# Reordering the front of a fused transformer step on Trainium2: x and modulation loads interleaved, five subtractions moved to GpSimd, zero products ahead of the constants

## The chip, the cores and the metric

The kernel runs on one core of one Trainium2 chip. Its time is the device time of one execution in microseconds (us), and the number to predict is the median over several executions. The engines are called by the profile's short names: PE is TensorE (PEld its weight loads), DVE is VectorE, ACT is ScalarE, POOL is GpSimd, SP is the engine that issues most DMAs. A name with q (ACTq, SPq) is an engine's instruction queue, as it issues a DMA.

## The reference, cut to what matters

One layer of a hybrid network over 640 tokens (128 context and 512 latent tokens) of width 1024, all in float32. The stages that the change touches are these:

```
m = silu(cond) @ w_mod + b_mod              # 2 conditionings, 1024 x 6144: shift, scale, gate (twice)
u = layer_norm(x) * (1 + scale) + shift     # 640 x 1024
z = u @ w_in                                # 1024 x 2816: q, k, v, recurrence, gate, Hyena
h = sin(freq0 * (feats @ w1 + b1))          # Hyena's filters: feats 640 x 33, w1 33 x 64
h = sin(freq1 * (h @ w2 + b2))              # w2 64 x 64
filters = (h @ w3) * exp(-t * |decay|)      # w3 64 x 1024; forward and backward half
spectrum = real Fourier transform of the circular filters
```

Behind them come the convolutions in the frequency domain, a recurrence, attention, the output projection and a mixture of 16 experts. They fill the time from about 65 us to the end and are the same in both kernels.

## The kernel before, in words

The core's engines run one hand-ordered program each; semaphores tie them together. Everything lives in one SBUF array called `arena`, so most names in the profile are `arena`; PSUM banks are called `bank`.

The front, up to about 65 us, does four things at once.

- **The filters.** PE makes layer 0 (`filter_layer(0)`, L1426, 33 rows by 64 columns), DVE folds its argument to the sine's range (`filter_fold`, L2052 to L2058), ACT takes the sine (L976), PE makes layer 1 (L1422), then fold and sine again. PE then makes five tiles of filter rows (`filter_rows`, L1456) into ten places in PSUM banks, some of them used twice. For each tile DVE runs `filter_parts(a)` (L2087 to L2100): the near half times a window into `EV`, the far half times a window into `OD`, after which `eo_win` counts one up, then EV = near + far and OD = near - far. Tiles 1 and 0 of the token order also get one more addition on a single partition (`skip`, L2100). The order of tiles is `FILTER_ORDER = (1, 2, 3, 4, 0)`.
- **The spectra.** `spectrum(g, odd)` (L1477) is two products of 128x128 by 128x512; DVE combines the halves in `spectrum_far` and `spectrum_near` (L2110, L2115).
- **The modulation.** SP loads eight blocks of `w_mod` (1024 KB each) through three buffers, and PE multiplies each block in `mod1(k)` (L1410). After the last one ACT and DVE copy the four result rows out of PSUM (L1013, L2142; semaphore `m1_ev`), and PE transposes them (L1525).
- **The normalisation.** `x_moments(i)` (L2077 to L2079) makes the mean and variance of token tile i on DVE, as soon as its rows have landed. ACT takes roots and scales x. PE transposes x (`ut`, L1438 and L1444), ACT applies scale and shift (L1021) and rounds to a high half (L1026), and DVE makes the low half (`u_low`, L2157).

PE's engine would be idle between these products, so `front_dense(n)` (L1491) inserts n products of the identity with constants; their results are never read. The first product of the input projection (`m = 0`, L1574 and L1575) waits per k for `u_low(k)`. GpSimd makes the low half of each weight piece (`low_half`, L772) from about 47 us on and has nothing to do between 3 and 47 us.

DVE waits in its own order: `filter_fold(0)`, `x_moments(0)`, `x_moments(1)`, `filter_fold(1)`, `x_moments(2..4)`, `filter_parts(0)`, `filter_parts(1)`, two tiny operations on the moments, `filter_parts(2..4)`. PE's `filter_rows([(3, 1)])` waits for `eo_win` 2, since the banks that it writes are read by `filter_parts` 0 and 1.

On the queues: SP issues `consts`, the five tiles of x, then the blocks of `w_mod`; ACT issues `filt` (features, w1 and w2 in one table of 128 partitions), `decay`, twice `hy_w3` and `skip`, later the transform's table `dft_taps`.

Of the kernel before, what the change touches and what calls it, by code (L numbers as in the profile page):

```python
# [9 lines left out]
P = 128  # L10
# [57 lines left out]
def build(nc, t):  # L68
# [8 lines left out]
    with ctx:  # L77
# [160 lines left out]
        filt = fl.take(NTOK + HIDDEN + P)  # L238
        feats, w1, w2 = filt[:, 0:NTOK], filt[:, NTOK:NTOK + HIDDEN], filt[:, NTOK + HIDDEN:NTOK + HIDDEN + P]
# [123 lines left out]
        mod_in = [sem(f"mod_in{i}") for i in range(3)]  # L363
        mod1_mm = sem("mod1_mm")
# [114 lines left out]
        modc_in = sem("modc_in")  # L479
# [21 lines left out]
        mod1_buf = [arena[:, MTAT:MTAT + 2048], arena[:, MTAT + 2048:MTAT + 4096], flat[1]]  # L501
        mod2_buf = [flat[1], flat[2], flat[0]]

        def wait_w_in(eng, p):

            eng.wait_ge(win_in[p % 2], 16 * (p // 2 + 1))
# [31 lines left out]
        def _(eng):  # L538
# [6 lines left out]
            for i in range(TT):  # L545
                eng.dma_start(X[:, i, :], t["x"][i * P:(i + 1) * P, :]).then_inc(ld_x[i], 16)
# [9 lines left out]
            def mod1_block(k):  # L556
                if k >= 3:
                    eng.wait_ge(mod1_mm, k - 2)
                eng.dma_start(mod1_buf[k % 3], t["w_mod"][k * P:(k + 1) * P, 0:2048]).then_inc(mod_in[k % 3], 16)
# [16 lines left out]
            for k in range(KT):  # L576
                mod1_block(k)
# [167 lines left out]
        def _(eng):  # L745
# [20 lines left out]

            def low_half(m):
# [175 lines left out]
        def _(eng):  # L943
# [11 lines left out]
            eng.dma_start(filt, t["filt"]).then_inc(ld_filt, 16)  # L955
# [55 lines left out]
            eng.wait_ge(eo_rdy, TT)  # L1011
            for g in range(2):
                S.activation(mrow1[g], mod_rows(B[4], g), ACT.Copy).then_inc(m1_ev, 1)  # L1013
# [390 lines left out]
        def _(eng):  # L1404
# [8 lines left out]
            def mod1(k):  # L1413

                eng.wait_ge(mod_in[k % 3], 16 * (k // 3 + 1))
                mod_block(B[4], k, mod1_buf[k % 3]).then_inc(mod1_mm, 1)

            def filter_layer(layer):
# [4 lines left out]
                else:  # L1423
                    eng.wait_ge(ld_filt, 16)
# [22 lines left out]
            eng.wait_ge(ld_const, 16)  # L1447
# [13 lines left out]
            def spectrum(g, odd):  # L1461
# [11 lines left out]
                else:  # L1473
                    eng.wait_ge(eo_win, (3, 3, 4)[g - 1])
                src, bank = (OD if q else EV), (odd_bank if odd else even_bank)[g]
# [5 lines left out]
            def ctx_spectrum():  # L1481

                eng.wait_ge(eo_rdy, TT)
                eng.wait_ge(half_ev, 4)
# [3 lines left out]
            def front_dense(n):  # L1488

                for b in range(n):  # L1490
                    mm(B[5][:, :], ident, consts[:, 2 * KT:2 * KT + 512], start=True, stop=True)  # L1491
# [25 lines left out]
            mod1(6)  # L1517
            mod1(7)
            spectrum(1, 1)
# [73 lines left out]
            def mod2(b):  # L1593

                eng.wait_ge(mod_in[b % 3], 16 * ((3, 3, 2)[b % 3] + b // 3 + 1))
# [431 lines left out]
        def _(eng):  # L2027
# [15 lines left out]
            ts_(cond, sig, 0.5, None, ALU.mult).then_inc(modc_in, 1)  # L2043
            after(modc_in)
# [36 lines left out]
            def filter_parts(a):  # L2081
# [5 lines left out]
                tt_(EV[:, i, :], b0[:, :], WN[:, i, 0:512], ALU.mult)  # L2087
                if i < 2:

                    stt(OD[:, i, :], b1[:, :], col("not0"), WN[:, i, 512:1024], ALU.mult, ALU.mult).then_inc(eo_win, 1)  # L2090
# [874 lines left out]
```

## Time and profile before

| | us |
|---|---|
| median of 3 runs | 634.93 (634.59 to 637.37) |
| the profiled execution, its own time | 633.17 |
| its span, first to last instruction | 631.3 |
| PE busy in the span | 600.8 |
| DVE, ACT, POOL busy | 440.5, 305.6, 188.4 |

The span begins with the first instruction of any engine. The profiled execution took 1.87 us more than its span. Times below are from the span's start.

### The profile page before, as it was taken

What the parts mean: (1) busy time and instruction counts of PE and PEld (TensorE: products, weight loads), DVE (VectorE), ACT (ScalarE), POOL (GpSimd) and SP (SyncE); (2) the same over time, 40 slices, a digit from 0 to 9 for tenths busy, and PEclk for the clock granted to TensorE, in tenths of its full rate; (3) what the DMA queues carried; (4) which work ended last, traced back from release to release, by engine and by line L of the source; (5) the groups of instructions that cost most, each with busy time, mean ns of one, the idle gap of its engine ahead of it and who ended that gap; (6) DMA issues with size and microseconds to landing.
All of it is one profiled execution on the core that took longest, in us unless ns stands there. A gap on an engine that the chain in (4) does not pass through costs nothing.

```text
span 631.3 us, 9327 instructions
## 1 busy us (share of the span) xinstructions
PE 600.8 (95%) x3353; PEld 455.3 (72%) x3353; DVE 440.5 (70%) x757; ACT 305.6 (48%) x506; POOL 188.4 (30%) x152
## 2 busy tenths in 40 slices
PE   6899999999999988998999999989999999999994
PEld 2237999999999965557888888747767677676352
DVE  4967766834994654467553499988998877983187
ACT  2748122335344543005795342846565655752354
POOL 1002333345551307041496070421212221321121
PEclk9999999999999999999999999999999999999998
DMA  9985852222221269764980706769999999999788
GB/s 305 387 305 222 305 186 97 101 101 100 101 68 66 92 238 325 303 264 99 290 271 36 294 8 234 280 168 370 393 376 403 390 388 406 374 364 372 291 299 144
DMA packets 40040, 154.89 MB, mean 245 GB/s; under 512 B 7049, under 2 KB 17033, under 8 KB 27451
## 3 DMA queue, kind: packets, MB, share of 16 engines
q1 hardware_dynamic: 27912, 115.41, 50.6%
q10 hardware_dynamic: 5522, 23.48, 9.4%
q0 software_dynamic: 6560, 15.42, 8.3%
q8 instruction: 27, 0.44, 0.3%
q14 instruction: 19, 0.15, 0.1%
HBM read 141.59 MB, written 23.63 MB: 262 GB/s over the span
## 4 chain that ended last, share of the span: by engine, by line
PE 82%; DVE 7%; DMA 5%; ACT 4%; issue 2%; POOL 0%; DVEq 0%; ACTq 0%; POOLq 0%
PE bank L1898 13%; PE bank L1574 12%; PE bank L1575 12%; PE bank L1770 9%; PE bank L1952 8%; PE bank L1410 3%; PE bank L1747 2%; PE bank L1674 2%; PE bank L1880 2%; DMA arena<-in_w_mod 2%; PE bank L1477 2%; PE bank L1625 2%; PE bank L2011 2%; PE bank L1730 2%; DMA u_scr<-arena 1%
## 5 line engine op out<-in xcount | busy, mean ns | idle before, releaser
L772 POOL TENSOR_TENSOR w_low<-arena,w_high 128x1024 fp32r<-128x1024 f32 x22 | 53.6, 2437 | 145.9 <-ACT w_high L971 145.9
L2544 DVE TENSOR_TENSOR gate_up_low<-arena,gate_up_high 128x1024 fp32r<-128x1024 f32 x64 | 75.3, 1221 | 12.3 <-ACT gate_up_high L1256 10.2
L1256 ACT ACTIVATE gate_up_high<-arena 128x1024 fp32r<-128x1024 f32 x64 | 63.9, 1054 | 15.5 <-DMA arena<-in_moe_w_gu 15.5
L971 ACT ACTIVATE w_high<-arena 128x1024 fp32r<-128x1024 f32 x22 | 23.2, 1058 | 87.8 <-PE bank L1575 87.0
L1574 PE MATMUL bank<-u_high,w_high 128*128 128x320 f32 x176 | 56.3, 320 | 1.7 <-DVE u_low L2157 1.7
L1952 PE MATMUL bank<-arena 128*128 128x512 f32 x128 | 57.7, 593 | 0.0
L1575 PE MATMUL bank<-u_high,w_low 128*128 128x320 f32 x176 | 54.4, 309 | 0.0
L1574 PE MATMUL bank<-u_high,w_low 128*128 128x320 f32 x176 | 54.4, 309 | 0.0
L1574 PE MATMUL bank<-u_low,w_high 128*128 128x320 f32 x176 | 54.4, 309 | 0.0
L1575 PE MATMUL bank<-u_low,w_high 128*128 128x320 f32 x176 | 54.4, 309 | 0.0
L1575 PE MATMUL bank<-u_high,w_high 128*128 128x320 f32 x176 | 54.4, 309 | 0.0
L1898 PE MATMUL bank<-gate_up_high,xt_high 128*128 128x512 f32 x128 | 51.4, 402 | 0.5 <-DVE xt_low L2696 0.5
L1898 PE MATMUL bank<-gate_up_low,xt_high 128*128 128x512 f32 x128 | 50.0, 391 | 0.0
L1898 PE MATMUL bank<-gate_up_high,xt_low 128*128 128x512 f32 x128 | 50.0, 390 | 0.0
L902 POOL DMA_INDIRECT y_scr<-arena,store_rows x16 | 17.7, 1108 | 84.2 <-DVE arena L2710 79.7
L1952 PEld LDWEIGHTS bank<-arena 128*128 128x128 f32 x128 | 23.2, 190 | 23.1 <-issue 23.0
L895 POOL DMA_INDIRECT arena<-u_scr,tokens x18 | 19.6, 1087 | 59.1 <-PE bank L1880 49.6
L1574 PEld LDWEIGHTS bank<-u_high,w_high 128*128 128x128 f32 x176 | 33.1, 188 | 2.9 <-DVE u_low L2157 2.6
L1575 PEld LDWEIGHTS bank<-u_high,w_high 128*128 128x128 f32 x176 | 33.1, 188 | 0.2 <-issue 0.2
L1574 PEld LDWEIGHTS bank<-u_low,w_high 128*128 128x128 f32 x176 | 33.0, 188 | 0.0
L1574 PEld LDWEIGHTS bank<-u_high,w_low 128*128 128x128 f32 x176 | 33.0, 188 | 0.0
L1575 PEld LDWEIGHTS bank<-u_low,w_high 128*128 128x128 f32 x176 | 33.0, 188 | 0.0
(442 smaller groups left out, 1396.4 us busy)
## 6 DMA issues: line engine op xcount, KB each, us to landing
arena<-in_moe_w_gu SPq DMA_DIRECT2D x38, 1024.0 KB, 10.1
arena<-in_w_mod SPq DMA_DIRECT2D x24, 1024.0 KB, 6.6
arena<-in_moe_w_down ACTq DMA_DIRECT2D x13, 1024.0 KB
arena<-in_w_in SPq DMA_DIRECT2D x11, 1024.0 KB, 4.8
arena<-in_moe_w_down SPq DMA_DIRECT2D x6, 1024.0 KB
y_scr<-arena SPq DMA_DIRECT2D x11, 512.0 KB, 9.1
arena<-in_x SPq DMA_DIRECT2D x10, 512.0 KB, 9.6
arena<-y_scr SPq DMA_DIRECT2D x10, 512.0 KB, 6.0
```

Of the source, the lines that this page charges most:

```text
L772: G.tensor_tensor(WL[s_][:, :, w], ring[s_][:, :, w], WH[m % 2].bitcast(F), ALU.subtract).then_inc(wl_rdy, 1)
L895: eng.indirect_dma_start(xg[j], None, u_scr, bass.IndirectOffsetOnAxis(ap=which, axis=0), bounds_check=NTOK - 1, oob_is_err=False).then_in ...
L902: eng.indirect_dma_start(y_scr, bass.IndirectOffsetOnAxis(ap=stores[:, n:n + 1], axis=0), yy[n % 2], None, bounds_check=2 * NTOK, oob_is_e ...
L971: S.activation(WH[m % 2], ring[(m // 2) % 2][:, :, (m % 2) * P:(m % 2 + 1) * P], ACT.Copy).then_inc(wh_rdy, 1)
L1256: S.activation(WGH[j][c], raw_gu[s][:, c, :, :], ACT.Copy).then_inc(wgh_rdy, 1)
L1410: last = mm(bank[32 * g:32 * g + 32, :], cond32[k], w[:, 512 * g:512 * (g + 1)], start=(k == 0), stop=(k == KT - 1))
L1574: mm(B[1 + m % 2][:, 0:HALF], w, u[k][:, HALF:NTOK], start=first, stop=end)
L1575: last = mm(B[3 + m % 2][:, 0:HALF], w, u[k][:, 0:HALF], start=first, stop=end)
L1770: last = mm(B[2 * (i % 2) + b][:, :], x[j][:, k, :], w[p][c][:, k % 2, :], start=(k == 0 and q == 0), stop=(k == KT - 1 and q == 2))
L1898: last = mm(B[j][:, :], x[j][:, k, :], w[k // 2][:, k % 2, :], start=(k == 0 and q == 0), stop=(k == KT - 1 and q == 2))
L1952: last = mm(B[4 + b][:, :], hT[j][:, k, :], raw_dn[s][:, k, b * 512:(b + 1) * 512], start=(k == 0), stop=(k == 1))
L2544: tt_(WGL[s][c], raw_gu[s][:, c, :, :], WGH[j][c].bitcast(F), ALU.subtract).then_inc(wgl_rdy, 1)
```

## The change

- SP's order: x tile 0, `w_mod` block 0, x tiles 1 and 2, block 1, x tiles 3 and 4, blocks 2 to 7. Five buffers instead of three (`mod1_buf`). The first two pieces of `w_in` wait for five and eight products of `mod1` (before: none and six).
- `filt` becomes 33 partitions by 704 columns, and w2 a transfer of its own (`hy_w2`, 128x128).
- `filter_parts` works in place in the window array `WN`, DVE keeps the sum, and the difference goes to GpSimd, with a new semaphore `od_rdy`.
- `x_moments(1)` comes after `filter_fold(1)`.
- PE begins with `front_zero(4)`: four products of the array ZERO with itself, 256 columns each, after the first `pads`; the wait for the constants stands behind them. Each f32 product is two records in the trace. `front_dense` is 3, 2 and (into bank 0, after `eo_win` 1) 1 instead of 1, 4 and 4. Each `mod1(0..2)` moves one place earlier; `mod1(7)` comes after `spectrum(1, 1)` instead of before it.
- At the end of `m = 0`, `u_low(6)` no longer stands behind `spectrum_far(3)`, nor `u_low(7)` behind `spectrum_near(3)`.

```diff
-        mod1_buf = [arena[:, MTAT:MTAT + 2048], arena[:, MTAT + 2048:MTAT + 4096], flat[1]]
+        mod1_buf = [arena[:, MTAT:MTAT + 2048], arena[:, MTAT + 2048:MTAT + 4096], flat[1], flat[2], flat[0]]
...
             eng.dma_start(consts, t["consts"]).then_inc(ld_const, 16)
-            for i in range(TT):
-                eng.dma_start(X[:, i, :], t["x"][i * P:(i + 1) * P, :]).then_inc(ld_x[i], 16)
...
             def mod1_block(k):
-                if k >= 3:
-                    eng.wait_ge(mod1_mm, k - 2)
+                if k >= 5:
+                    eng.wait_ge(mod1_mm, k - 4)
...
             def w_in_piece(p):
-                if p == 1:
-                    eng.wait_ge(mod1_mm, 6)
+                if p < 2:
+                    eng.wait_ge(mod1_mm, 8 if p else 5)
...
-            for k in range(KT):
+            for i in range(TT):
+                x_rows(i)
+                if i in (0, 2):
+                    mod1_block(i // 2)
+            for k in range(2, KT):
                 mod1_block(k)
...
+            for a in range(TT):
+                i = FILTER_ORDER[a]
+                eng.wait_ge(eo_win, a + 1)
+                G.tensor_tensor(OD[:, i, :], WN[:, i, 0:512], WN[:, i, 512:1024], ALU.subtract).then_inc(od_rdy, 1)
...
-            eng.dma_start(filt, t["filt"]).then_inc(ld_filt, 16)
+            eng.dma_start(filt[0:FEATS, :], t["filt"]).then_inc(ld_filt, 16)
+            eng.dma_start(w2, t["hy_w2"]).then_inc(ld_filt, 16)
...
-            front_dense(1)
+            front_zero(4)
+            eng.wait_ge(ld_const, 16)
             filter_layer(0)
-            front_dense(4)
+            front_dense(3)
             filter_layer(1)
-            eng.wait_ge(modc_in, 1)
-            front_dense(4)
+            eng.wait_ge(cond_rdy, 2)
+            mod1(0)
+            front_dense(2)
             eng.wait_ge(filt_sin, 2)
             eng.wait_ge(ld_tables, 64)
             filter_rows([(0, 0), (1, 1)])
-            mod1(0)
+            mod1(1)
             eng.wait_ge(filt_read, 2)
             filter_rows([(2, 1), (4, 0)])
-            mod1(1)
+            mod1(2)
+            eng.wait_ge(eo_win, 1)
+            front_dense(1, 0)
             eng.wait_ge(eo_win, 2)
             filter_rows([(3, 1)], 2)
-            mod1(2)
             spectrum(0, 0)
...
             spectrum(0, 1)
             mod1(6)
+            spectrum(1, 1)
             mod1(7)
-            spectrum(1, 1)
...
-                tt_(EV[:, i, :], b0[:, :], WN[:, i, 0:512], ALU.mult)
+                near, far = WN[:, i, 0:512], WN[:, i, 512:1024]
+                tt_(near, b0[:, :], near, ALU.mult)
...
-                    tt_(OD[:, i, :], b1[:, :], WN[:, i, 512:1024], ALU.mult).then_inc(eo_win, 1)
+                    tt_(far, b1[:, :], far, ALU.mult).then_inc(eo_win, 1)
                 after(eo_win)
-                step(tt_(EV[:, i, :], EV[:, i, :], OD[:, i, :], ALU.add))
-                if i < 2:
-                    eng.wait_ge(ld_tables, 64)
-                last = stt(OD[:, i, :], OD[:, i, :], -2.0, EV[:, i, :], ALU.mult, ALU.add)
+                last = tt_(EV[:, i, :], near, far, ALU.add)
                 if i < 2:
                     step(last)
+                    eng.wait_ge(ld_tables, 64)
                     last = tt_(EV[0:1, i, :], EV[0:1, i, :], skip[0:1, :], ALU.add)
...
-            x_moments(1)
             filter_fold(1)
-            for i in range(2, TT):
+            for i in range(1, TT):
                 last = x_moments(i)
...
-                if k == 7:
-                    spectrum_far(3)
             u_low(KT - 2)
+            spectrum_far(3)
+            u_low(KT - 1)
             spectrum_near(3)
-            u_low(KT - 1)
```

## Rows read from the trace of the kernel before

**Rows 1.** The page: busy time, share of the span, and instructions of PE, PEld, DVE.
```profile
PE 600.8 (95%) x3353; PEld 455.3 (72%) x3353; DVE 440.5 (70%) x757; ACT 305.6 (48%) x506; POOL 188.4 (30%) x152
```

**Rows 2.** The chain that ended last, 0 to 80 us: start, length, what.
```profile
0.72 3.98 DMA arena<-in_consts
...
8.29 5.74 PE bank L1491 x8
...
22.15 0.69 DVE arena L2087
...
27.04 1.98 PE bank L1456 x4
...
30.02 1.91 PE bank L1477 x4
...
42.38 1.85 PE bank L1410 x16
...
46.14 0.35 PE bank L1525 x16
```

**Rows 3.** DMA issues between 3.8 and 4.5 us: count, size, median time to landing.
```profile
arena<-in_w_mod SPq DMA_DIRECT2D x1, 1024.0 KB, 16.6
...
arena<-in_w_mod SPq DMA_DIRECT2D x2, 1024.0 KB, 17.8
```

**Rows 4.** Stretches: engines' busy time, clock, DMA share, last column GB/s.
```profile
0.00:21.20 21.20, 15.98 (x40) 5.76 (x40) 12.62 (x30) 7.88 (x10) 1.70 (x17) 1.00 0.93 336
...
15.60:25.50 9.90, 9.42 (x38) 2.73 (x36) 9.49 (x19) 7.59 (x9) 0.00 (x0) 1.00 1.00 425
```

**Rows 5.** Timelines of SP's queue and of DVE up to 26 us: start, length.
```profile
3.89 34.05 SPq L559 DMA_DIRECT2D arena<-in_w_mod  x8
...
8.41 0.68 DVE L2052 TENSOR_SCALAR arena<-bank,arena 128x384 f32<-128x384 f32 x1 [2.28 <-PE bank L1426]
...
17.80 0.69 DVE L2077 BATCH_NORM_STATS2 arena<-arena 128x6 f32<-128x512 f32 x1
...
23.53 0.69 DVE L2094 TENSOR_TENSOR arena<-arena 128x512 f32<-128x512 f32 x1
...
24.98 0.68 DVE L2100 TENSOR_TENSOR arena<-arena 1x512 f32<-1x512 f32 x1
```

**Rows 6.** Timeline, stretches in which POOL and DVE both work.
```profile
47.37 4.68 POOL L772 TENSOR_TENSOR w_low<-arena,w_high 128x1024 fp32r<-128x1024 f32 x2 [44.36 <-ACT w_high L971]
...
47.69 0.69 DVE L2115 TENSOR_TENSOR arena<-arena,bank 128x512 f32<-128x512 f32 x1
...
111.66 2.42 POOL L772 TENSOR_TENSOR w_low<-arena,w_high 128x1024 fp32r<-128x1024 f32 x1 [5.17 <-ACT w_high L971]
...
111.78 2.31 DVE L2296 TENSOR_TENSOR arena<-arena 128x4 f32<-128x4 f32 x1
```

**Rows 7.** Groups of POOL instructions by line and shape: busy us, mean ns.
```profile
L803 POOL TENSOR_TENSOR arena<-arena 128x1024 f32<-128x1024 f32 x8 | 18.8, 2355 | 21.6 <-DMA arena<-in_rpb 21.5
...
L815 POOL TENSOR_TENSOR arena<-arena 128x256 f32<-128x256 f32 x10 | 7.3, 728 | 0.8
```

**Rows 8.** Timeline of PEld, front_dense(4): start, length.
```profile
11.79 0.34 PEld L1491 LDWEIGHTS bank<-arena 128*128 128x128 f32 x1 [0.52 <-issue]
12.58 0.19 PEld L1491 LDWEIGHTS bank<-arena 128*128 128x128 f32 x1 [0.45 <-issue]
```

**Rows 9.** Timeline, around the last mod1 block and the spectrum's halves.
```profile
42.51 0.69 DVE L2110 TENSOR_TENSOR arena<-arena,bank 128x512 f32<-128x512 f32 x1 [4.55 <-PE bank L1477]
...
44.37 1.42 DVE L2142 COPY arena<-bank 2x512 f32<-2x512 f32 x2 [0.45 <-PE bank L1410]
```

**Rows 10.** Timeline at the end of m = 0.
```profile
61.44 0.74 ACT L1026 ACTIVATE u_high<-arena 128x640 fp32r<-128x640 f32 x1
...
62.45 0.82 DVE L2157 TENSOR_TENSOR u_low<-arena,u_high 128x640 fp32r<-128x640 f32 x1
...
64.79 0.19 PEld L1574 LDWEIGHTS bank<-u_high,w_high 128*128 128x128 f32 x1 [0.58 <-DVE u_low L2157]
```

More of the change, by code:

```diff
@@ L237, in build @@
         HF, FA, FB = (fl.take(SPAN) for _ in range(3))
-        filt = fl.take(NTOK + HIDDEN + P)
-        feats, w1, w2 = filt[:, 0:NTOK], filt[:, NTOK:NTOK + HIDDEN], filt[:, NTOK + HIDDEN:NTOK + HIDDEN + P]
+        filt = fl.take(NTOK + HIDDEN)
+        feats, w1 = filt[:, 0:NTOK], filt[:, NTOK:NTOK + HIDDEN]
+        w2 = fl.take(P)
         decay = fl.take(D)
@@ L363, in build @@
         mod_in = [sem(f"mod_in{i}") for i in range(3)]
+        mod1_in = mod_in + win_in
         mod1_mm = sem("mod1_mm")
@@ L478, in build @@
         scalar_st = sem("scalar_st")
-        modc_in = sem("modc_in")
+        od_rdy = sem("od_rdy")
         eo_win = sem("eo_win")
@@ L556, in mod1_block @@
             def mod1_block(k):
-                if k >= 3:
-                    eng.wait_ge(mod1_mm, k - 2)
-                eng.dma_start(mod1_buf[k % 3], t["w_mod"][k * P:(k + 1) * P, 0:2048]).then_inc(mod_in[k % 3], 16)
+                if k >= 5:
+                    eng.wait_ge(mod1_mm, k - 4)
+                eng.dma_start(mod1_buf[k % 5], t["w_mod"][k * P:(k + 1) * P, 0:2048]).then_inc(mod1_in[k % 5], 16)
             def w_in_piece(p):
-                if p == 1:
-                    eng.wait_ge(mod1_mm, 6)
+                if p < 2:
+                    eng.wait_ge(mod1_mm, 8 if p else 5)
                 elif p >= 2:
@@ L1011, in _ @@
             eng.wait_ge(eo_rdy, TT)
+            eng.wait_ge(od_rdy, TT)
             for g in range(2):
@@ L1474, in spectrum @@
                     eng.wait_ge(eo_win, (3, 3, 4)[g - 1])
+                if q:
+                    eng.wait_ge(od_rdy, 4 if odd else 2)
                 src, bank = (OD if q else EV), (odd_bank if odd else even_bank)[g]
@@ L1483, in ctx_spectrum @@
                 eng.wait_ge(eo_rdy, TT)
+                eng.wait_ge(od_rdy, TT)
                 eng.wait_ge(half_ev, 4)
@@ L1486, in ctx_spectrum, with front_dense, front_zero @@
                 mm(B[3][:, :], TAPSc[1], OD[:, 0, :], start=True, stop=True).then_inc(spec_mm, 1)
-            def front_dense(n):
+            def front_dense(n, bank=5):
                 for b in range(n):
-                    mm(B[5][:, :], ident, consts[:, 2 * KT:2 * KT + 512], start=True, stop=True)
-            front_dense(1)
+                    mm(B[bank][:, :], ident, consts[:, 2 * KT:2 * KT + 512], start=True, stop=True)
+            def front_zero(n):
+                eng.wait_ge(pads, 1)
+                for b in range(n):
+                    mm(B[5][:, 0:256], ZERO[:, 0:P], ZERO[:, 0:256], start=True, stop=True)
+            front_zero(4)
+            eng.wait_ge(ld_const, 16)
             filter_layer(0)
-            front_dense(4)
+            front_dense(3)
             filter_layer(1)
-            eng.wait_ge(modc_in, 1)
-            front_dense(4)
+            eng.wait_ge(cond_rdy, 2)
+            mod1(0)
+            front_dense(2)
             eng.wait_ge(filt_sin, 2)
@@ L2042, in _ @@
             step(stt(sig, sig, 1.0, cond, ALU.add, ALU.mult))
-            ts_(cond, sig, 0.5, None, ALU.mult).then_inc(modc_in, 1)
-            after(modc_in)
+            ts_(cond, sig, 0.5, None, ALU.mult).then_inc(cond_rdy, 1)
+            eng.wait_ge(cond_rdy, 2)
             magic = 1.5 * 2.0 ** 23
@@ L2140, in _ @@
             eng.wait_ge(mod1_mm, KT)
+            eng.wait_ge(od_rdy, TT)
             for g in range(2, 4):
@@ L2909 @@
     pair2[0:HIDDEN, 0:HIDDEN] = pair2[HIDDEN:P, HIDDEN:P] = a["hy_w2"][0]
-    filt = np.zeros((P, NTOK + HIDDEN + P), f32)
-    filt[0:FEATS, 0:NTOK] = features()
-    filt[0:FEATS, NTOK:NTOK + HIDDEN] = a["hy_w1"][0]
-    filt[:, NTOK + HIDDEN:] = pair2
+    filt = np.concatenate([features(), a["hy_w1"][0]], 1).astype(f32)
     rgw = np.zeros((P, 8, P), f32)
```

17 lines of the change are left out of this document (9 added, 8 removed).

## The prediction

> **What bounds the kernel now.** I read the page first, then the chain that ended last for the first 80 us, then the timelines of the engines in that stretch, then the DMA issues. PE is busy for 95% of the span [rows 1], and nothing behind 65 us is edited, so only what the front does to the start of the projections counts. The reader should see three stretches in the chain [rows 2]: until 14 us PE (the constants at 4.70, then among others eight filler records that end at 14.03 and hold up layer 1); until 27.04 DVE, which has no gap; and from 27.04 to 46.14 PE again, 19.10 us without a gap. Behind it, ACT's chain over eight values of k and DVE's low halves set the end of m = 0 [rows 10]. I sum the change as a shift of each of these marks.
>
> **Where DVE starts its filter parts (T0, before 22.15) [rows 2].** In the new order DVE does four tiles of moments after the second fold, and the last needs x tile 4. Three tiles took 17.80 to 22.15 without a gap [rows 2, 5], so one takes 1.45, and nothing waited for x.
>
> - By engines alone: POOL's first memsets end about 2 us into the span. Four zero products are eight records of 256 columns. The eight filler records of 512 columns took 5.74 [rows 2]: about five at 0.86 and three at 0.43, since PE's records became twice as fast between the loads at 11.79 and 12.58 [rows 8], near 12.4. So 256 slow columns are 0.43, the zeros 3.4 us, to 5.5. Layer 0 takes 1.5 more (constants plus filler to the next filler, 4.70 to 8.29, less 2.07), a fold and sine 3.7 (the fold began at 8.41 [rows 5]; the sine was done near 12.0), so layer 1 could run at 10.7 and end at 11.5 if PE is fast by then. A fold of 3.1 and four tiles of 5.8 give T0 = 20.4. If PE stays slow until 12.4 as before, three fillers (5.2 us) end at 12.3, layer 1 at 13.1, and T0 = 22.0.
> - By the queue: x tile 4 now stands behind two blocks of w_mod. Exactly the same bytes of SP's queue (constants, five tiles, two blocks) were through when the second block landed before. The first block was issued at 3.89 [rows 5] and took 16.6, the median of the first two is 17.8 [rows 3], so the second, issued some 0.35 later, took 19.0 and landed at about 23.2. The filter's table shrinks from 416 KB to 91, plus 64 for w2: 261 KB less, 0.6 us at 425 GB/s [rows 4]. Late bound: 22.6. The early bound counts bytes only: SP's 5.0 MB and ACT's 2.1 MB make 7.1 MB, which the DMA engines had moved by 21.2 [rows 4]. I take the middle, 21.9; with 1.45 for its moments T0 = 23.35.
>
> The later of the two decides: T0 moves by +1.2. The earlier filter layers, the zero products among them, are then hidden behind the wait for x tile 4; if x came in time they would be worth the 1.6 between 22.0 and 20.4.
>
> **DVE and POOL (eo_win 2, before 27.04).** Before, near, far, sum, difference, skip row, near, far took 4.87 from T0. Sum and difference together took 1.45 from 23.53 to 24.98 [rows 5]; without the difference it is 4.87 - 0.72 = 4.15. But POOL's subtraction runs at the same time. Its duration is not in the trace; between 728 ns for 256 columns and 2355 for 1024 [rows 7] 512 columns are 1.27. And DVE stands still meanwhile: while POOL worked from 111.66 to 114.08, a DVE addition of four columns took 2.31 and ended at 114.09; one that reads PSUM took its usual 0.69 at 47.69, within a POOL operation from 47.37 on [rows 6]. So products with a bank are free, the sum and the skip row are not. After far, DVE's own next instruction starts within some 0.04 (0.69 of a step of 0.72 is work), while POOL must be woken by another engine's semaphore. So I let DVE have the sum first, POOL follows, and the skip row waits for its end: about 1.2 us more, once before eo_win 2. If POOL went first, the cost is the same once, and 0.6 to 1.3 for each later tile, where PE is the bound and hides it. The bounds are 0 and 1.3; I take 1.15, since the nearest rows are unambiguous. From T0 to eo_win 2: 5.3 instead of 4.87, +0.4. So eo_win 2 comes at 28.65, +1.6.
>
> The Trainium skill speaks against this part too: its page GPSIMD Engine Reference, section Specifications, says that GpSimd shares its SBUF interfaces with VectorE, with contention for DVE instructions that have two SBUF inputs or run in a two-port mode. It gives no price. The four-column addition of 2.31 us [rows 6] agrees; with the rule but a price of nothing the sum would come out 1.15 lower, with the rows it is as above.
>
> **PE from eo_win 2 to the transposes (before 19.10) [rows 2].** mod1(2) now stands ahead of the wait: its block is behind x tile 4 in the queue, about 24.5 to 25, and the filler of 0.86 follows it, so both end before 28.65: -1.0. spectrum(1, 1) comes after one block of mod1 instead of two, and needs DVE's two halves of spectrum 0, the first of which began at 42.51 and took 0.69, after a product that ended at 42.38 [rows 2, 9]: 1.6 from that end, against 0.93 of mod1(6): +0.65, and the 0.93 of mod1(7) goes behind it. There the rows' copies follow: from mod1(7)'s end at 44.23 DVE copied until 45.79 [rows 2, 9], hidden by 1.91 of spectrum(1, 1); now nothing is left to hide them, and PE waits about 1.7. In all: rows 1.98, spectra and blocks to the end of spectrum(0, 1) 12.4 (30.02 to 42.38 [rows 2]), then 1.6, 1.9, 0.9, 1.7 = 20.45, +1.35. The marks behind shift by 1.6 + 1.35 = +2.95. The waits for od_rdy cost nothing: POOL's second difference is done about 3 us after eo_win 2, and the first odd product comes 5 us after it.
>
> **The end of m = 0.** Before, u_low(6) stood behind spectrum_far(3), and u_low(7) behind both halves, so k = 7 began on PE at 64.79 [rows 10]. ACT had its last high half at 62.18 (61.44 + 0.74), and with 0.82 for u_low(7) [rows 10] and 0.06 for the wake-up PE could begin at 63.06: -1.73. PE's own products reach this point at about 63.2, and start a little earlier relative to ACT than before, since u_low(0) no longer runs beside POOL's second low half. So I count the whole -1.73; if PE is the later one it is -1.6.
>
> **Edits at nothing.** The semaphore under mod1(0) is another name for the same event. SP's five buffers, the waits of w_in (piece 0 is issued after five blocks, as late as before, and wanted 3 us later; piece 1 some 5 us later than before, but not wanted until m = 0 has ended near 66 [rows 10]) and the move of filter fillers are hidden; if a w_in piece were late, ACT's high half would wait for it.
>
> **Sum.** +2.95 - 1.73 = +1.2. The profiled execution's own time is 633.17, of which 631.3 is span; the change would make it 634.4. The median shown is 1.76 above it, and on that scale the forecast is 634.93 + 1.2 = 636.1. Its own bounds: x tile 4 between 21.2 and 22.6 is -0.7 and +0.7, POOL's price -1.15 and +0.15, the copies +-0.3: 634.0 to 637.5.
>
> **Rivals.** (a) *The x tiles come in time*, because the small ACT transfers are shorter and share less. T0 = 20.4, eo_win 2 at 25.7, shift -1.35 + 1.35 = 0, and the sum is -1.7: 633.2, or 632.1 if POOL's price falls away too. For it: DVE and PE stand ready. Against it: the position in the queue. (b) *POOL costs nothing* with x late: +0.05, 635.0. Against it speak the rows cited. (c) *PE falls back to the slow level*, the rival on the slower side. The granted clock reads 1.00 throughout [rows 4], yet the filler's records took 0.86 until about 12.4 and 0.43 after it, which is the step from 1.2 to 2.4 GHz [rows 2, 8]; PE had been busy from 4.7 until it rose. Before, PE was busy for 9.42 of the 9.90 us from 15.60 on [rows 4]. Now I expect two gaps of about 2.5 us, from 17.4 to the landing of block 1 near 19.9 and from 22.3 to eo_win 1 near 24.7. If the clock falls there and needs as long as at the start, 7.7 us at half speed cost 3.85 behind eo_win 2: +5.1, 640.0. It decides when the level is still low at eo_win 2; a fall that is over by then costs nothing. For it: the gaps; against it: block 1 and the filler after eo_win 1 lie between. (d) *The zero products don't raise the clock.* T0 is then 22.0 by engines, still before 23.35: the same 636.1, and in case (a) 634.8.
>
> **Chances.** Forecast, with (d) in it, 0.48; (a) 0.24; (b) 0.12; (c) 0.11; 0.05 for others of either sign. About 0.5%, 3.2 us, is what a measurement of this kernel tells from no change. Of (a) and the rest 0.07 go below -3.2 us; of (c), the forecast's tail and the rest 0.13 go above +3.2. So 0.80 for no difference. The range from 632.3 to 638.6 leaves out about 0.08 below and 0.12 above.
>
> **What would show it.** Right: x tile 4 lands between 21 and 23, DVE has a gap before its last moments, and filter_parts(0) starts near 23; the two skip rows on DVE take 1.8 us instead of 0.68; PE waits 1.5 or more before L1525; u_low(6) and u_low(7) precede the halves of spectrum 3, with no wait of PE over 0.3 near the end of m = 0. Wrong: no wait for x, sums on DVE unchanged beside POOL, or records of 0.86 after 20 us.

## The result, and the profile after

| | before | after |
|---|---|---|
| median, 10 runs each on the same chip | 635.19 (633.47 to 637.37) | 639.33 (637.28 to 644.42) |
| ratio after/before, 95% interval | | 1.0069 (1.005 to 1.0087) |
| the profiled execution, its own time | 633.17 | 639.24 |
| its span | 631.3 | 637.2 |
| mean granted clock of the profiled execution | 0.997 | 0.99 |
| mean granted clock over all its executions (before: the 85 of the experiments) | 0.993 | 0.989 |

The change makes the kernel 4.1 us slower. The forecast was +1.2, and its range ended at 638.6. The engines' busy time on the page hardly differs from [rows 1]; only POOL has 10 us more:

```profile
PE 602.2 (95%) x3355; PEld 456.4 (72%) x3355; DVE 438.5 (69%) x752; ACT 305.5 (48%) x506; POOL 199.0 (31%) x157
```

The loss is mostly in waiting, and the same marks as before show where (us from the start of the span; k = 7 is the last product pair of m = 0):

| mark | before | forecast | after |
|---|---|---|---|
| T0, first `filter_parts` | 22.15 | 23.35 | 24.66 |
| eo_win 2 | 27.0 | 28.65 | 29.7 |
| third tile of filter rows | 27.04 | 28.65 | 30.8 |
| transposes of the modulation rows | 46.1 | 49.0 | 51.4 |
| k = 7 of m = 0 | 64.79 | 66.0 | 68.61 |

At k = 7 the kernel is 3.8 us behind, nearly all of the median's 4.1. The two profiled spans differ by 5.9; but the execution of before that was profiled lies 2.0 under its own median and that of after only 0.1. The other 2 us come behind m = 0, where the programs are the same: from k = 7 to PE's last product it takes 557.1 us before and 559.0 after, at a clock of 1.00 in both. In the profiles of the experiments this stretch takes between 556.2 and 559.8, so 2 us is within what single executions scatter.

The chain of work that ended last, from the first DMA issue to k = 7 (start, length, what), is to be held against [rows 2]:

```profile
3.72 17.96 DMA arena<-in_x
21.70 0.69 DVE arena L2102
...
24.66 0.69 DVE arena L2113
...
26.07 1.42 PE bank L1469 x2
...
30.84 1.91 PE bank L1469 x4
...
48.71 1.04 PE bank L1424 x8
49.83 0.69 DVE arena L2166
50.55 0.71 DVE arena L2166
51.39 0.41 PE bank L1550 x16
...
68.65 0.37 PE bank L1599
```

Before, the constants and PE's fillers led this chain. Now a transfer of x does, issued at 3.72 and landed at 21.70. It is x tile **3**; tile 4, issued at 4.3, follows 18.6 us later, near 22.9. Two tiles of moments (2.9 us) then stand between the landing and T0. The timeline of DVE shows the wait, the moments, and what became of sum and skip row:

```profile
21.70 0.69 DVE L2102 BATCH_NORM_STATS2 arena<-arena 128x6 f32<-128x512 f32 x1 [1.79 <-DMA arena<-in_x]
...
24.66 0.69 DVE L2113 TENSOR_TENSOR arena<-bank,arena 128x512 f32<-128x512 f32 x1
...
26.05 0.69 DVE L2120 TENSOR_TENSOR arena<-arena 128x512 f32<-128x512 f32 x1
26.77 1.63 DVE L2124 TENSOR_TENSOR arena<-arena 1x512 f32<-1x512 f32 x1
...
49.83 1.42 DVE L2166 COPY arena<-bank 2x512 f32<-2x512 f32 x2 [3.18 <-PE bank L1424]
```

The skip row takes 1.63 us instead of 0.68 [rows 5], beside POOL's difference:

```profile
26.10 1.76 POOL L777 TENSOR_TENSOR arena<-arena 128x512 f32<-128x512 f32 x1 [23.09 <-DVE arena L2116]
```

POOL's record ends at 27.86, DVE's at 28.40, 0.54 behind it: the row began at 26.77, and the records look as if it did its work once POOL was done. This is the lock that the prediction described.

PE's granted clock in stretches of 5 us (after the stretch and its length: busy time of PE, PEld, DVE, ACT, POOL, then the clock, the DMA share and GB/s):

```profile
10.00:15.00 5.00, 5.00 (x15) 1.56 (x14) 4.35 (x9) 0.52 (x1) 0.00 (x0) 0.69 1.04 315
20.00:25.00 5.00, 2.53 (x14) 0.68 (x6) 3.19 (x7) 4.98 (x7) 0.00 (x0) 1.00 1.03 428
25.00:30.00 5.00, 3.93 (x11) 1.00 (x12) 4.86 (x7) 0.89 (x2) 1.96 (x2) 0.68 1.01 428
30.00:35.00 5.00, 5.00 (x14) 1.51 (x16) 4.79 (x9) 3.31 (x3) 3.36 (x2) 0.98 1.01 426
```

Before, the clock read 1.00 throughout [rows 4], and on to PE's last product. (It reads 1.00 in the slow start of either program too; there the length of the records tells.) Now PE falls to the low level twice, and each fall has an idle stretch ahead of it. The timeline of PE has both:

```profile
2.07 3.78 PE L1513 MATMUL bank<-arena 128*128 128x256 f32 x8 [2.07 <-POOLq L768]
7.90 0.86 PE L1440 MATMUL bank<-arena 33*64 33x384 f32 x4 [2.05 <-DMA arena<-in_hy_w]
...
26.07 1.42 PE L1469 MATMUL bank<-arena 64*128 64x512 f32 x2 [3.54 <-DVE arena L2116]
27.41 1.94 PE L1424 MATMUL bank<-arena 128*32 128x512 f32 x8
29.28 1.55 PE L1507 MATMUL bank<-arena 128*128 128x512 f32 x2
30.77 0.69 PE L1469 MATMUL bank<-arena 64*128 64x512 f32 x1
```

The first idle stretch is new: the zero products end at 5.85, and layer 0 then waits 2.05 us for w2, which is now a transfer of its own in the same semaphore. In the seven other kernels with this table, profiled once each, layer 0 began between 5.75 and 6.25, so this stretch belongs to this one execution. The second lasts 3.54 us, while DVE waits for x. Behind it mod1(2) takes 1.94 and the filler 1.55, where 1.0 and 1.1 are usual, so the third tile of filter rows starts 1.05 us after the bank that it wants is free.

### The profile page after: what moved, and what is told of

Read it like the earlier page. It is cut to its first block, busy times and chain, and to the rows that moved or that the text cites. A ratio compares the mean times of both kernels' runs of the same rounds, so it can differ in the third digit from the quotient of the medians.

```text
span 637.2 us, 9336 instructions
## 1 busy us (share of the span) xinstructions
PE 602.2 (95%) x3355; PEld 456.4 (72%) x3355; DVE 438.5 (69%) x752; ACT 305.5 (48%) x506; POOL 199.0 (31%) x157
## 4 chain that ended last, share of the span: by engine, by line
PE 73%; DMA 13%; DVE 7%; ACT 4%; issue 3%; SPq 0%; DVEq 0%; POOL 0%; POOLq 0%; ACTq 0%
PE bank L1599 12%; PE bank L1600 12%; PE bank L1923 11%; PE bank L1795 9%; PE bank L1977 6%; DMA arena<-in_w_mod 3%; PE bank L1424 3%; DMA arena<-in_x 3%; DMA arena<-in_moe_w_gu 2%; PE bank L1772 2%; PE bank L1699 2%; PE bank L1492 2%; PE bank L1905 2%; PE bank L2036 2%; DVE gate_up_low L2567 1%
## 5 line engine op out<-in xcount | busy, mean ns | idle before, releaser
L914 POOL DMA_INDIRECT y_scr<-arena,store_rows x16 | 18.6, 1160 | 89.0 <-DVE arena L2733 82.7
## 6 DMA issues: line engine op xcount, KB each, us to landing
arena<-in_moe_w_gu SPq DMA_DIRECT2D x38, 1024.0 KB, 13.5
arena<-in_moe_w_down SPq DMA_DIRECT2D x6, 1024.0 KB, 10.9
```

The lines of the kernel that those rows point to most:

```text
L914: eng.indirect_dma_start(y_scr, bass.IndirectOffsetOnAxis(ap=stores[:, n:n + 1], axis=0), yy[n % 2], None, bounds_check=2 * NTOK, oob_is_e ...
```

## The experiments

x_first, warm, mod7_ahead and no_zeros ran on one chip together; tail_only, zeros_tail, mixed and no_pool on a second; warm_mod7, zeros_only and ones_lead on a third. The medians of the kernel before on the three were 635.11, 635.18 and 635.28 (27 to 29 runs each). Ratios are to it; marks are from one profiled execution of each kernel. An interval of a ratio is 1.1 to 1.7 us wide to either side, so of two kernels of the table a difference under about 2 us isn't established by the medians alone.

| kernel | median | ratio (95%) | mean clock | T0 | transposes | k = 7 |
|---|---|---|---|---|---|---|
| x_first | 636.41 | 1.0011 (0.9988 to 1.0035) | 0.9887 | 21.33 | 48.95 | 66.17 |
| warm | 638.51 | 1.0062 (1.0041 to 1.0083) | 0.9918 | 24.48 | 50.23 | 68.27 |
| mod7_ahead | 637.17 | 1.0043 (1.0017 to 1.0069) | 0.9877 | 24.49 | 49.97 | 67.2 |
| warm_mod7 | 634.16 | 0.9983 (0.996 to 1.0006) | 0.9935 | 24.53 | 47.69 | 64.93 |
| mixed | 632.41 | 0.9961 (0.9942 to 0.998) | 0.9937 | 20.75 | 44.91 | 62.13 |
| no_zeros | 638.65 | 1.0068 (1.0041 to 1.0095) | 0.9891 | 24.47 | 51.19 | 68.41 |
| no_pool | 638.92 | 1.0064 (1.0042 to 1.0085) | 0.9893 | 24.42 | – | – |
| tail_only | 633.69 | 0.9983 (0.9959 to 1.0008) | 0.9928 | 22.10 | 47.62 | 65.30 |
| zeros_only | 632.96 | 0.996 (0.9934 to 0.9986) | 0.9936 | 20.89 | 46.47 | 65.22 |
| ones_lead | 633.48 | 0.998 (0.9955 to 1.0005) | 0.9939 | 20.76 | 44.69 | 63.66 |
| zeros_tail | 631.59 | 0.9942 (0.9926 to 0.9959) | 0.9941 | 20.18 | 44.11 | 61.55 |

The mean clock needs care, since it counts stretches in which the level costs nothing. Behind PE's last product the level falls in every profile; the last stretch of before, then of after:

```profile
625.00:631.30 6.30, 0.00 (x0) 0.00 (x0) 2.35 (x4) 1.02 (x3) 0.00 (x0) 0.65 0.76 166
630.00:637.20 7.20, 0.00 (x0) 0.00 (x0) 3.03 (x7) 1.53 (x3) 0.35 (x1) 0.56 0.67 146
```

PE has no product in either. One minus the clock, times the length of the stretch, is the full-speed time that the low level takes: 2.2 us here before and 3.2 after, from 2 to 3.2 in all the kernels. The same sum over the stretches up to 80 us tells of the front: 0 in the profiles of before, zeros_tail, ones_lead, mixed and warm_mod7; 1.7 in tail_only, zeros_only, warm and no_zeros; 3.4 in after, x_first and mod7_ahead; 8.5 in no_pool.

### x_first: is it the place in the queue?

After, with all of x ahead of the blocks, and mod1(0) to mod1(2) at their old places on PE.

```diff
             for i in range(TT):
                 x_rows(i)
-                if i in (0, 2):
-                    mod1_block(i // 2)
-            for k in range(2, KT):
+            for k in range(KT):
                 mod1_block(k)
```

> The changed kernel with the five x tiles ahead of all blocks of w_mod, and with mod1(0), mod1(1), mod1(2) back at their old places, since their blocks land later. Theory 1 (the late x tiles hold DVE): no wait of DVE for x, filter_parts(0) begins near 21 instead of 24.66, the third row tile (L1469 after eo_win 2) near 26.5 instead of 30.77, the transposes near 48 (the third block is back behind the rows, +1.0), and the time is 2.5 to 3.5 us under the changed kernel's, about 1 above that of before. Rival (something else, such as POOL's lock or the clock, makes the front late): filter_parts(0) earlier, but the rows after eo_win 2 not before 29.

The median is 2.9 us under that of after, and k = 7 comes 2.4 us earlier. DVE no longer waits for x, and T0 comes 3.3 us earlier. But now the first block is late. PE's timeline and the stretch around it:

```profile
20.70 1.94 PE L1422 MATMUL bank<-arena 128*32 128x512 f32 x8 [1.79 <-DMA arena<-in_w_mod]
...
20.00:25.00 5.00, 4.30 (x16) 1.24 (x16) 4.86 (x7) 4.47 (x6) 1.76 (x1) 0.58 1.01 426
```

PE stood idle from 14.2 to 16.2 and from 18.9 to 20.7 and fell to the low level near 17.4, between the two, this time ahead of eo_win 2 instead of behind it. The mean clock over the runs, 0.9887, is as low as that of after. So the place of x in the queue, with the places of the three blocks on PE that go with it, is worth about 3 us here, and with x in time the rest of the change is still no gain.

### warm: fill PE's second gap

```diff
             eng.wait_ge(filt_read, 2)
+            front_dense(4, 6)
             filter_rows([(2, 1), (4, 0)])
```

> The changed kernel with four more filler products (into bank 6) ahead of filter_rows 2 and 4, so that PE isn't idle in front of the first eo_win. Theory 2 (PE's low level after idle time costs about 1 us): the granted clock stays at 1.00 from 20 us on, the row tile, block and filler after the first eo_win take about 2.8 us instead of 4.7, the third row tile starts at eo_win 2 (29.8) instead of 30.77, and the time is 1.0 us lower. Rival (the low level costs nothing, since DVE is the later one): clock 1.00, but the third row tile still near 30.8 and the same time.

It gains 0.8 us, within the intervals. The fillers do what they are for: the clock holds at 1.00 from 20 to 50 us, and the third tile of filter rows starts at 29.61, 1.2 earlier. Then the level falls elsewhere. In PE's stretch behind the transposes:

```profile
50.00:55.00 5.00, 4.77 (x30) 3.32 (x31) 2.26 (x8) 3.50 (x5) 4.03 (x2) 0.68 0.89 264
```

PE had waited 1.69 us for the rows' copies, with mod1(7)'s end ahead of it, and the level fell near 51.8, some 1.6 us after PE had started again. x's transposes then ran at half speed:

```profile
50.23 0.42 PE L1551 MATMUL bank<-arena 2*128 2x2 f32 x16 [1.69 <-DVE arena L2167]
...
53.38 1.92 PE L1458 MATMUL bank<-arena 128*128 128x128 f32 x8
```

### mod7_ahead: give the rows' copies their cover back

```diff
+            mod1(7)
             spectrum(1, 1)
-            mod1(7)
```

> The changed kernel with mod1(7) ahead of spectrum(1, 1) again. Theory 3 (the uncovered copies of the modulation rows and the wait for DVE's halves cost 2.3 us): PE has no gap of over 0.3 us between spectrum(0, 1) and the transposes, these start 2.3 to 2.5 us earlier (near 49.0 instead of 51.39), and the time is 2.3 us lower. Rival (the later marks absorb it, as ACT's high halves wait for w_in or for PE anyway): the transposes come earlier, but the first product of m = 0 moves by less than 1.

It gains 2.2 us, and the intervals of the two just overlap. From the third tile of filter rows to the transposes it takes 18.21 us instead of 20.62, since no wait is left there:

```profile
46.20 1.92 PE L1424 MATMUL bank<-arena 128*32 128x512 f32 x16
48.05 1.98 PE L1492 MATMUL bank<-arena 128*128 128x512 f32 x4
49.97 0.41 PE L1550 MATMUL bank<-arena 2*128 2x2 f32 x16
```

mod1(6) and mod1(7) run together, spectrum(1, 1) hides the copies, and the transposes follow without a gap. In its profile the level was low for longer at the same place as in after, 25 to 35 us, which is why the transposes came at 49.97 and not near 49.0:

```profile
25.00:30.00 5.00, 4.11 (x11) 0.94 (x12) 4.86 (x7) 0.00 (x0) 2.13 (x2) 0.53 1.02 429
30.00:35.00 5.00, 5.00 (x9) 1.77 (x10) 4.29 (x8) 3.49 (x4) 3.18 (x2) 0.79 1.02 429
```

### warm_mod7: both repairs of PE, x still late

The two edits above together.

> The changed kernel with both repairs on PE's side, the four fillers ahead of filter_rows 2 and 4 and mod1(7) ahead of spectrum(1, 1); x tiles stay late. If the three causes add up, the third row tile starts near 29.6, the transposes near 47.8, and the time is 3.3 to 3.5 us under that of the changed kernel, near 636.0. What is left between it and the kernel of x tiles first with the same order at the end of the blocks (632.4) is then the late x tiles, 3.5 us. Rival (PE idle behind mod1(7) and the low level are the same loss seen twice): 637 as with mod1(7) alone.

T0 is as late as in after (24.53), and yet the kernel takes 634.16, which is 5.2 us less than after and not to be told from before. The level does not fall; of the stretches from 20 to 55 us the two that fell above now read

```profile
25.00:30.00 5.00, 4.45 (x19) 1.26 (x16) 4.86 (x7) 0.00 (x0) 2.09 (x2) 1.00 1.01 428
...
50.00:55.00 5.00, 5.00 (x34) 3.96 (x33) 2.72 (x5) 4.78 (x7) 2.96 (x2) 1.00 1.04 385
```

This run shows that most of the loss can be had back while x stays late. It doesn't show that late x is free: the kernel keeps the new end of m = 0, which tail_only puts at 1.5, and only with that does it come out level with before. At k = 7 it is 3.7 us ahead of after: 0.1 from T0, 1.0 from there to the third row tile, 2.6 from there to the transposes. The mean clock rises from 0.989 to 0.9935 (0.0045 of 639 is 2.9 us, part of it where it costs nothing), and the way from the third row tile to the transposes shortens from 20.62 to 18.04. The expectation was 636.0, so the gain is larger than forecast. Alone the two repairs gained 0.8 and 2.2; that together they gain 2.2 more than this sum is in line with the traces (with either alone the level still fell in the front), but the four medians have uncertainties of 1.2 to 1.7 each, so the excess itself is not established.

### mixed: x in time as well

x_first and mod7_ahead together, x_moments(1) ahead of `filter_fold(1)` as before, and two more fillers behind layer 1:

```diff
-            front_dense(2)
+            front_dense(4)
...
             x_moments(0)
+            x_moments(1)
             filter_fold(1)
-            for i in range(1, TT):
+            for i in range(2, TT):
```

> The changed kernel without the parts that the runs so far showed to cost: x tiles ahead of the blocks, mod1(0..2) at their old places, mod1(7) ahead of spectrum(1, 1), x_moments(1) between the folds, four fillers behind layer 1. The zeros, five buffers, the small filter table, POOL's differences, the filler after eo_win 1 and the new end of m = 0 stay. If the causes are the late x tiles, the order at the end of the blocks and the low level, filter_parts(0) begins near 20.5, the third row tile near 25.6, the transposes near 44.8, and the time is 2.5 to 3 us under that of before (ratio 0.9955). Rival (a cause not found stays in): not faster than before.

632.41, faster than before. Against warm_mod7, whose clock is the same, this leaves 1.7 us for the late x and the few places on PE and DVE that go with it, where 3.5 were expected. The intervals of the two overlap; the marks put k = 7 at 62.13 against 64.93, 2.8 earlier.

### no_zeros: after without the leading products

```diff
-            front_zero(4)
             eng.wait_ge(ld_const, 16)
```

> The changed kernel without its four zero products: PE begins with layer 0, when the w2 table has landed near 7.9. Theory 4 (the zero products raise PE's level before layer 0, but the gain is hidden behind the x tiles): layer 0 takes 1.5 us instead of 0.86, layer 1 ends some 0.5 to 1 later, DVE still waits for x tile 3 at 21.7, filter_parts(0) begins at 24.7 as before, and the time is that of the changed kernel within 0.5 us. Rival (the zeros do nothing to the level): layer 0 takes 0.86 all the same. Second rival (the early start costs: an early rise lets the level fall again before 13 us): the products at 26 to 31 us run at the high level now, and the time is 1 us lower.

638.65: no difference from after. Layer 0 runs at 5.75 and at half speed, layer 1 ends near 13.5, and still T0 is 24.47, because x tile 3 lands as late:

```profile
5.75 1.54 PE L1440 MATMUL bank<-arena 33*64 33x384 f32 x4 [5.75 <-DMA arena<-in_hy_w]
```

Here layer 0 has to wait for the same transfer, but to 5.75, not 7.90. When w2 lands varies from one execution to another: in mod7_ahead, whose program is that of after up to 40 us, layer 0 began at 5.78 right behind the zeros.

### no_pool: the differences back on DVE

```diff
-            for a in range(TT):
-                i = FILTER_ORDER[a]
-                eng.wait_ge(eo_win, a + 1)
-                G.tensor_tensor(OD[:, i, :], WN[:, i, 0:512], WN[:, i, 512:1024], ALU.subtract).then_inc(od_rdy, 1)
...
-                last = tt_(EV[:, i, :], near, far, ALU.add)
+                step(tt_(EV[:, i, :], near, far, ALU.add))
+                last = stt(OD[:, i, :], far, -2.0, EV[:, i, :], ALU.mult, ALU.add)
...
                 after(eo_rdy)
+                eng.sem_inc(od_rdy, 1)
```

> The changed kernel with the five differences back on DVE, everything else as it is. Theory 5 (POOL's lock gives back what the moved work saves): the skip row takes 0.68 instead of 1.63 and the difference 0.72, so from filter_parts(0) to eo_win 2 it is 4.9 instead of 5.1, DVE ends its last tile some 2 us later than now, which PE does not wait for, and the time is that of the changed kernel within 0.5 us. Rival (the lock is a main part of the loss): the time falls by 1 us or more.

638.92 against 639.33: the same. From T0 to eo_win 2 it is 5.02 us, with POOL it was 5.06. DVE's timeline for the first tile, against that of after above:

```profile
26.53 0.69 DVE L2117 SCALAR_TENSOR_TENSOR arena<-arena 128x512 f32<-128x512 f32 x1
27.26 0.68 DVE L2121 TENSOR_TENSOR arena<-arena 1x512 f32<-1x512 f32 x1
28.15 0.69 DVE L2109 TENSOR_TENSOR arena<-bank,arena 128x512 f32<-128x512 f32 x1 [0.21 <-DVE arena L2121]
```

The difference costs 0.69 on DVE, and the skip row is back at 0.68. From the first near product to that of the next tile it is 3.73 us; with POOL it was 3.78. The lock is real, and in this tile it eats the whole of what the move saved. It doesn't in every tile: where DVE's next work reads a bank, as in after's third tile, the near products of two tiles are 2.05 us apart (31.63 to 33.68) and were 2.78 before. But there PE is the later one. (The profiled execution of no_pool took 643.72, with a clock of 0.53 from 25 to 37 us; its marks behind eo_win 2 are left out for that.)

### tail_only: before, with the new order at the end of m = 0

```diff
-                if k == 7:
-                    spectrum_far(3)
             u_low(KT - 2)
-            spectrum_near(3)
+            spectrum_far(3)
             u_low(KT - 1)
+            spectrum_near(3)
```

> The kernel before with the new order of u_low(6), u_low(7) and spectrum 3's halves alone. Theory 6: k = 7 of m = 0 begins 1.5 to 1.7 us earlier than 64.79 and all behind it too; time 1.5 us under that of before (ratio 0.9976). Rival (the shift is taken up by the next waits, for POOL's and ACT's halves of m = 1): marks behind m = 1 unmoved.

633.69, or 1.5 us less, with an interval that just reaches no change. From the first product of m = 0 to k = 7 it takes 10.44 us instead of 11.99, and PE now waits 0.22 there and not 0.58 [rows 10]:

```profile
65.30 0.19 PEld L1574 LDWEIGHTS bank<-u_high,w_high 128*128 128x128 f32 x1 [0.22 <-DVE u_low L2157]
```

k = 7 itself is no earlier than before, since in this execution the clock read 0.85 and 0.81 from 25 to 35 us. The order of x and the blocks is that of before here, so a fall of the level is no speciality of the new order. In the front it fell in two of the five profiles with the order of before (tail_only and zeros_only), and in all six with the new program and at least one of PE's gaps open.

### zeros_only, ones_lead, zeros_tail: the leading products where x doesn't bind

zeros_only is before with four zero products in place of the first filler; ones_lead has products of ones instead, from a buffer that GpSimd fills; zeros_tail is zeros_only with tail_only's edit.

```diff
-            front_dense(1)
+            eng.wait_ge(pads, 1)
+            for b in range(4):
+                mm(B[5][:, 0:256], ZERO[:, 0:P], ZERO[:, 0:256], start=True, stop=True)
+            eng.wait_ge(ld_const, 16)
             filter_layer(0)
...
-            eng.wait_ge(ld_const, 16)
             def filter_rows(tiles, tail=1):
```

> The kernel before with the four zero products in place of the first filler, nothing else. Against zeros and new end of m = 0 together (ratio 0.9942) and the new end alone (0.9983), the zeros alone should give 0.996: filter_parts(0) between 20.2 and 21.3 instead of 22.15, depending on the moment of the rise. Rival (the gain came from the pair only): within 0.1% of before.

> As the zeros alone, but the four leading products are of ones with ones (a memset of 128x256 more on GpSimd ahead of them, 0.3 us). If PE's level follows the instructions and not the numbers, the level rises as with zeros, 6 to 11 us into the span, and the time is that of the zeros within 0.3 us more. Rival (zeros count less, since nothing switches): the rise is regularly earlier with ones, near 6, and the time lower by 0.5 to 1.5 us.

> The kernel before with the four zero products in front instead of one filler, and the new order at the end of m = 0. Theory: zeros end near 5.8, layer 0 by 7.3, four fillers by 12 to 14 depending on when the level rises, so layer 1 ends 0 to 1.5 earlier than 14.7, filter_parts(0) 0 to 1.3 earlier than 22.15; with the 1.5 of the end of m = 0 the time is 1.5 to 2.8 us under that of before. Rival (the zeros don't count for the level, only their time): nothing beyond the 1.5.

zeros_only is 2.3 us faster than before, outside the interval; ones_lead is 1.8 faster, its interval just reaching no change. (In zeros_only's profile the level fell near 28, and its k = 7 is no earlier than before's; the gain rests on the medians.) The two are 0.5 apart and not to be told from each other. zeros_tail is the fastest kernel of the study, 3.6 us under before, where at most 2.8 were expected, and 7.7 under after. In its profile layer 0 and the eight fillers, the first work behind the zeros, ran at the high level from near 6 us on:

```profile
5.79 0.97 PE L1426 MATMUL bank<-arena 33*64 33x384 f32 x4
6.69 3.70 PE L1490 MATMUL bank<-arena 128*128 128x512 f32 x8
```

The same eight took 5.74 before [rows 2]. In after, too, layer 0 took 0.86 at 7.90, with nothing but zeros ahead of it on PE, where it took 1.54 in no_zeros. In no_pool the zeros themselves took 3.51 instead of 3.78 us: the level rose before they had ended, with nothing else ahead on PE.

```profile
2.08 3.51 PE L1509 MATMUL bank<-arena 128*128 128x256 f32 x8 [2.08 <-POOLq L768]
```

Products of zeros thus count for the level. They don't fix the moment: with the same head of the program the level rose near 6 us in zeros_tail and near 10.9 in zeros_only; with ones it rose near 7. Even in zeros_only T0 is 1.3 us earlier than before, of which about 1.0 is that layer 0 begins at 5.78 and not at 6.75, since no filler stands ahead of it. A kernel without the first filler and without zeros wasn't run, so how much of the 2 us is the level and how much the missing filler stays open.

## Why the prediction was wrong

Two steps failed. The landing of x was put too early, which cost 1.3 us at T0; and PE's level was put at nothing in the sum, as a rival with a chance of 0.11, where its fall cost at least 1.05 us ahead of the third row tile. Either alone would have left the time inside the range. The other steps came out as they stood, within 0.3 us.

**The steps of the whole difference.** Three kernels between before and after make a ladder, whose steps add up to +4.1:

| from | to | us | what |
|---|---|---|---|
| before | zeros_tail | -3.6 | leading zeros and the new tail |
| zeros_tail | mixed | +0.8 | what is left of the new front, POOL among it; within the intervals |
| mixed | warm_mod7 | +1.7 | x behind the blocks (and the places of mod1(0..2), x_moments(1) and a few fillers); within the intervals, 2.8 at k = 7 |
| warm_mod7 | after | +5.2 | PE's gaps: its level, and the uncovered copies |

Of the last step the prediction had the copies (2.4 of it) and not the level. That leaves 2.8 us for the level by the medians, uncertain by about 2, and 1.0 by the marks.

**T0: failed; the mechanism right, the term mis-sized.** "I take the middle, 21.9; with 1.45 for its moments T0 = 23.35": x did come late and DVE did wait. But tile 4 landed at 22.9, beyond the late bound of 22.6: 1.0 of the 1.3. And the step looked only at the last tile. Tile 3, right ahead of it in the same queue, landed at 21.70; with two tiles of moments of 1.45 it decides, at 24.66, 0.3 later than tile 4 alone would have it. T0 moved by 2.5 instead of 1.2. The early bound, which counted bytes at the full rate over both queues, carried the middle away from the better-founded late one.

**POOL: right.** The skip row took 1.63 where the forecast had 1.8, and T0 to eo_win 2 took 5.06 where it had 5.3. The lock cost 0.95 on the skip row (1.63 against 0.68), the move saved 0.7 on DVE, and no_pool shows that they cancel to within 0.05 in the first tile. Rival (b) falls as a statement on the lock. The 1.63 agrees with the Trainium skill's rule, on the page GPSIMD Engine Reference, section Specifications, that the two engines share SBUF interfaces, with contention for VectorE's instructions that have two SBUF inputs.

**The row tile to the transposes: right.** 20.62 us measured, 20.45 forecast. DVE's copies, begun at 49.83, lie bare (PE waits 1.69 for them, 1.7 forecast), and mod7_ahead and warm_mod7 give 2.4 and 2.6 back.

**The end of m = 0: right.** From the transposes to k = 7 it is 17.22, where before has 18.71: -1.5, against -1.73. PE's last wait there is 0.22, as forecast under 0.3:

```profile
68.61 0.19 PEld L1599 LDWEIGHTS bank<-u_high,w_high 128*128 128x128 f32 x1 [0.22 <-DVE u_low L2181]
```

**PE's level: failed, put at nothing.** Rival (c), "PE falls back to the slow level", had 0.11 and the sentence "against it: block 1 and the filler after eo_win 1 lie between". They did not hold the level. It fell behind the 3.54 us of idle time and was low, by the records, until near 30; the third row tile started 1.05 us after eo_win 2. The rival's own sum went wrong the other way: a full 7.7 us at half speed behind eo_win 2, 640.0. In the profiled execution it cost about 1.0 there, and the other fall, from 9.7 to 13.1, nothing that shows, since DVE waited for x. What the prediction had no place for is that a fall is a matter of frequency: the mean clock over all runs is 0.989 with either order of x while both gaps are open, and 0.9935 with both filled. Before's is 0.993, not 1: its profiled execution, 0.997, on which "reads 1.00 throughout" rested, was one of the better ones. In full-speed time, median times one minus the mean clock, that is 7.0 us in after and 4.5 in before. The difference of 2.5 us is no price: 2 to 3 us of each lie behind PE's last product, some in gaps that nothing waits for, and mod7_ahead has a lower mean clock than after (0.9877) and is the faster one.

**By marks.** T0 +1.3 beyond the forecast, POOL -0.2, the low level at the third row tile +1.05, the stretch to the transposes +0.2, the tail +0.2: 2.5 of the 2.6 us by which k = 7 was later than forecast. The time was 3.2 over the forecast. Of the 0.6 between, 0.3 is that the median of before, from which the forecast counted, was 634.93 with three runs and 635.19 with ten; 0.3 is what the medians differ by beyond k = 7. The mean clock isn't added to this; part of it is in these marks. One slip in the recorded sum: its own upper bounds add up to 637.3, not 637.5.

**The other rivals.** (a), x in time, is what x_first builds, and it does not reach 633.2: T0 was 21.33 instead of 20.4, and the first block took the place of x as the late transfer, with its own gap on PE. (d), that zeros don't raise the clock, falls by zeros_tail and no_pool; that an early rise does not matter in after while x binds is shown by no_zeros. The prediction's zeros "to 5.5" ended at 5.85, but layer 0 then waited to 7.90 for w2. "Layer 0 takes 1.5 more" counted no transfer; with x late this cost nothing.

**Still open.** At what moment the level rises after a start or falls after a gap differs between executions of programs with the same head, and one profile per kernel can't give the distribution. Nor was it settled how much of the 5.2 us between warm_mod7 and after is the level alone. The copies are some 2.4; the marks give the level 1.0; the mean clock (2.9, 0.0045 of 639) can't decide, since it counts time that nothing waits for.

## What to carry to other kernels

When transfers change places in one queue, work out every transfer's landing and what is still to be done behind each, not only the last one's. A wait on one engine leaves holes on another: list the holes in TensorE's program and price its clock there by several executions, since filling one hole while another stays open gave back little (0.8 us), and that together with the copies' cover 5.2. Read the clock by stretches and not by its mean, which counts time in which TensorE has nothing to do. Leading products in place of the first filler were worth about 2 us, but only where what they speed up is what the next stage waits for.

## What the runs showed of the hardware

- Products of zeros can raise TensorE's level: in no_pool the eight records of zeros took 3.51 us instead of 3.78, and eight filler records took 3.70 us behind zeros in zeros_tail, 3.70 behind ones, and 5.74 without either; but in zeros_only they took 5.52, with the same program head as in zeros_tail.
- The level can fall when PE is busy again: in after it stood at full in the stretch 20 to 25 us, with PE idle from 22.5 to 26.07, and then mod1(2), from 27.41, took 1.94 instead of 1.0; in warm it fell about 1.6 us after the end of a wait of 1.69.
- The level falls at the end of every profile, behind TensorE's last product: 0.65 over before's last 6.3 us, 0.56 over after's last 7.2, with no product in either.
- A VectorE addition of a single partition beside a GpSimd operation took 1.63 us instead of 0.68, though it has 512 elements only. VectorE's operations with a bank as an input took their usual 0.69 beside GpSimd. GpSimd's own difference of 512 columns is recorded with 1.76 us, of which the first 0.64 lie beside VectorE's sum (26.10 to 26.74), so alone it would take about 1.1, an estimate from these two records.
